# The second feed forward of a two-block model as seven block products per block, with the fifteen sums on VectorE

## The reference

```python
SEQ, D_MODEL, D_FF = 512, 1024, 4 * D_MODEL
for layer in range(2):
    ...
    h = _rmsnorm(x, norm_g[layer, 1]) * (1.0 + scale_f) + shift_f
    x = x + gate_f * (jnp.square(jax.nn.relu(h @ w_fc1[layer])) @ w_fc2[layer])
return _rmsnorm(x, norm_f)
```

## Time and profile before

| | us |
|---|---|
| median of 3 runs | 3584.62 |
| lowest, highest | 3583.39, 3584.72 |
| the profiled execution's own time | 3582.96 |
| its span in the profile | 3581.2 |
| TensorE busy | 3211.5 (90% of the span) |
| VectorE busy | 1821.2 (51%) |
| ScalarE busy | 697.5 (19%) |

### The profile page before, as it was taken

One profiled execution on the slowest core, in us unless ns is written; L12 is line 12 of the kernel. 1 busy time (PEld: TensorE's weight loads), 2 busy tenths in 40 slices (PEclk: granted clock), 3 DMA queues, 4 the chain that ended last, 5 costly groups with the idle time before them and its releaser, 6 DMA issues. The chain is left out here.

```text
span 3581.2 us, 27361 instructions
## 1 busy us (share of the span) xinstructions
PE 3211.5 (90%) x9960; PEld 1497.2 (42%) x9960; DVE 1821.2 (51%) x3995; ACT 697.5 (19%) x1519; POOL 653.9 (18%) x649
## 2 busy tenths in 40 slices
PE   8999799888888878787877899999999889999998
PEld 3454454333333333333333335444444475444443
DVE  5565831577766777677775237436544383111000
ACT  2133220222222222222221221112100232100000
POOL 0110100244444444444444000000000000000000
PEclk9999899999999899999899999999999999999999
DMA  5643411699999999999999122023444352112221
GB/s 196 233 159 105 153 59 59 257 422 417 421 407 406 421 421 422 421 421 421 412 418 418 67 112 71 36 85 115 184 158 145 148 207 98 62 66 75 80 73 71
DMA packets 118663, 799.00 MB, mean 223 GB/s; under 512 B 13728, under 2 KB 16416, under 8 KB 31872
## 3 DMA queue, kind: packets, MB, share of 16 engines
q0 software_dynamic: 91312, 619.09, 42.9%
q1 hardware_dynamic: 27216, 178.15, 13.7%
HBM read 767.83 MB, written 29.36 MB: 223 GB/s over the span
## 5 line engine op out<-in xcount | busy, mean ns | idle before, releaser
L1278 PE MATMUL po<-pair,diag 128*128 128x512 f32 x2048 | 988.1, 640 | 224.9 <-ACT diag L1338 224.7
L1425 DVE SCALAR_TENSOR_TENSOR pair<-pair,h_tm 128x1024 f32<-128x1024 f32 x512 | 616.2, 1224 | 298.7 <-DMA pair<-in_peer_uv,idx 295.2
L1198 POOL DMA_INDIRECT pair<-in_peer_uv,idx x512 | 581.5, 1136 | 964.1 <-PE po L1278 670.1
L1278 PEld LDWEIGHTS po<-pair,diag 128*128 128x128 f32 x2048 | 410.6, 205 | 781.5 <-issue 486.4
L1571 PE MATMUL acc<-a,ring 128*128 128x512 f32 x1024 | 441.7, 592 | 0.0
L1556 PE MATMUL acc<-hT,ring 128*128 128x512 f32 x960 | 412.3, 592 | 0.0
L1571 PEld LDWEIGHTS acc<-a,ring 128*128 128x128 f32 x1024 | 194.6, 190 | 244.9 <-issue 244.9
L1556 PEld LDWEIGHTS acc<-hT,ring 128*128 128x128 f32 x960 | 182.4, 190 | 229.6 <-issue 229.6
L1332 ACT ACTIVATE ge<-a 128x4 f32<-128x4 f32 x128 | 26.3, 205 | 895.9 <-DVE pair L1425 895.8
L1614 DVE SCALAR_TENSOR_TENSOR xT<-acc,mod,xT 128x512 f32<-128x512 f32 x16 | 12.0, 751 | 348.2 <-PE acc L1571 348.2
L1603 DVE TENSOR_TENSOR a<-a 128x512 f32<-128x512 f32 x64 | 43.6, 691 | 261.0 <-ACT a L1582 259.8
(11 more groups left out here) (405 smaller groups left out, 3213.3 us busy)
## 6 DMA issues: line engine op xcount, KB each, us to landing
ring<-in_w_fc SPq DMA_DIRECT2D x62, 1024.0 KB, 4.8
mg<-in_ada_w POOLq DMA_DIRECT2D x96, 512.0 KB, 5.2
s_tables<-table POOLq DMA_DIRECT2D x16, 1664.0 KB, 6.5
tab<-s_tables SPq DMA_DIRECT2D x16, 1664.0 KB, 6.4
ring<-in_w SPq DMA_DIRECT2D x15, 1024.0 KB, 4.9
first<-in_w_first SPq DMA_DIRECT2D x14, 1024.0 KB, 5.4
other<-in_w_first SPq DMA_DIRECT2D x14, 1024.0 KB, 5.0
pair<-in_peer_uv,idx POOLq DMA_INDIRECT x512, 14.6
```

The lines of the kernel that those rows point to most:

```text
L1198: pool.indirect_dma_start(out=pair[:, at, :], out_offset=None, in_=core.dram["peer_uv"][:, :], in_offset=bass.IndirectOffsetOnAxis(ap=idx[ ...
L1278: last = pe.matmul(po[:, t % 2, half * 512:(half + 1) * 512], diag[:, at, :], pair[:, at, D + half * 512:D + (half + 1) * 512], start=firs ...
L1425: dve.scalar_tensor_tensor(row, row, 1.0, h_tm[:, t, :], ALU.mult, ALU.mult, accum_out=a[:, g, s:s + 1]).then_inc(dotted, 1)
```

## The change

The stage is replaced by `feed_forward_halves`. Each product is treated as a product of 2x2 blocks: the weight matrix is halved by rows and by columns, the tokens' matrix is halved by features (tiles 0 to 3 and 4 to 7 of `hT`, or the two halves of a group of 8 tiles of `a`) and by tokens (0 to 255, `lo`, and 256 to 511, `hi`). Seven products of blocks take the place of eight. For that, four sums of weight blocks are made per chunk (`Halves.add`), four sums of token blocks per tile (`th` for the first product; `t` and, in place, the `hi` half of `a` for the second), and seven sums of results per tile. All of these run on VectorE. All matmuls of the stage have 256 columns.

One unit `p` of the first product is one chunk: seven groups of four matmuls, into two banks `x` and `y` of which each half is a result of its own. ScalarE copies `x` and `y` to `px` and `py` before the first half of each is accumulated further, and takes the third result straight into `a`. The ReLU moves into VectorE's squaring: `max(a, 0) * a`. In the second product four chunks make one unit `j`, which gives two output tiles, `j` and `4 + j`.

The weights are laid out on the host in another order (`by_halves`), again in chunks of 1 MB, and are issued by `Feed.load` (L341) by the same rule as before.

```diff
 class Sums:
...
-        act.activation(self.sq[:, k % 2, :], self.core.xT[:, k, :], ACT.Square).then_inc(self.squared, 1)
+        act.activation(self.sq[:, k % 2, :], self.core.xT[:, self.order[k], :], ACT.Square).then_inc(self.squared, 1)
...
+class Halves:
...
+    def add(self, dve, c):
+
+        if c >= 2:
+            dve.wait_ge(self.made, c - 1)
+        w = self.feed.chunk(dve, c, True)
+        a11, a12, a21, a22 = (w[:, i * 512:(i + 1) * 512] for i in range(4))
+        s = [self.sums[:, c % 2, i, :] for i in range(4)]
+        dve.tensor_tensor(s[0], a21, a22, ALU.add).then_inc(self.ready, 1)
+        dve.wait_ge(self.ready, 4 * c + 1)
+        dve.tensor_tensor(s[1], s[0], a11, ALU.subtract).then_inc(self.ready, 1)
+        dve.tensor_tensor(s[2], a11, a21, ALU.subtract).then_inc(self.ready, 1)
+        dve.wait_ge(self.ready, 4 * c + 2)
+        dve.tensor_tensor(s[3], a12, s[1], ALU.subtract).then_inc(self.ready, 1)
...
+def feed_forward_halves(core, layer, following):
+
+    N1, HT = FF // P, FF // P // 2
...
+        sums = Sums(core, st, st.ps("ms", [P, S])[:, :], sq=sq)
+        sums.order = [0, 4, 1, 5, 2, 6, 3, 7]
...
+        @block.tensor
+        def _(pe):
+            def seven(out, weight, tokens, first, start, stop=True):
+                for k in range(4):
+                    last = pe.matmul(out, weight(k), tokens(k), start=(start and k == 0), stop=(stop and k == 3), skip_group_check=True)
+                return last
+
+            for p in range(HT):
+                x, y = bank[:, 2 * (p % 2), :], bank[:, 2 * (p % 2) + 1, :]
...
+                feed.chunk(pe, p, True)
+                if p == 0:
+                    pe.wait_ge(products.ready, 4)
+                if p >= 2:
+                    pe.wait_ge(c_taken, p - 1)
+                seven(x[:, lo], block_(0), lambda k: core.hT[:, k, lo], True, True)
+                pe.wait_ge(halves.ready, 4 * p + 2)
+                if p == 0:
+                    pe.wait_ge(t_ready, 2)
+                seven(x[:, hi], sum_(2), lambda k: th[:, 1, k, :], True, False).then_inc(x_made, 1)
+                if p >= 2:
+                    pe.wait_ge(y_taken, p - 1)
+                seven(y[:, lo], sum_(1), lambda k: th[:, 0, k, :], True, True)
+                pe.wait_ge(halves.ready, 4 * p + 3)
+                if p == 0:
+                    pe.wait_ge(t_ready, 3)
+                seven(y[:, hi], sum_(3), lambda k: core.hT[:, k, hi], True, False).then_inc(y_made, 1)
+                pe.wait_ge(x_copied, p + 1)
+                seven(x[:, lo], block_(1), lambda k: core.hT[:, 4 + k, lo], False, False).then_inc(z_made, 1)
+                pe.wait_ge(halves.ready, 4 * p + 4)
+                pe.wait_ge(y_copied, p + 1)
+                seven(y[:, lo], sum_(4), lambda k: core.hT[:, 4 + k, hi], False, False)
+                if p == 0:
+                    pe.wait_ge(t_ready, 4)
+                seven(y[:, hi], block_(3), lambda k: th[:, 2, k, :], False, False).then_inc(made, 1)
+
+            for j in range(4):
...
+                for kk in range(4):
+                    n = HT + 4 * j + kk
...
+                    if kk == 0 and j >= 2:
+                        pe.wait_ge(x_copied, HT + j - 1)
+                        pe.wait_ge(y_copied, HT + j - 1)
+                        pe.wait_ge(z_copied, j - 1)
...
+                    if kk == 0 and j:
+                        pe.wait_ge(added, 2 * j)
+                    seven(last_half, block_(3), lambda k: t[:, 2, at + k, :], True, start).then_inc(made, 1)
+                    if kk == 1 and j:
+                        sums.add(pe, 2 * j - 2)
+                    if kk == 2 and j:
+                        sums.add(pe, 2 * j - 1)
+            sums.add(pe, KT - 2)
+            sums.add(pe, KT - 1)
+
+        @block.scalar
+        def _(act):
...
+            for p in range(HT):
...
+                act.wait_ge(x_made, p + 1)
+                if p:
+                    act.wait_ge(a_ready, p)
+                copy(px[:, :, :], two(x), x_copied)
+                act.wait_ge(y_made, p + 1)
+                copy(py[:, :, :], two(y), y_copied)
+                act.wait_ge(z_made, p + 1)
+                copy(a[:, p, lo], x[:, lo], c_taken)
...
+        @block.vector
+        def _(dve):
...
+            products.vector(dve)
+            halves.add(dve, 0)
+            h = core.hT
+            dve.wait_ge(products.ready, KT)
+            sub(th[:, 0, :, :], h[:, 0:4, hi], h[:, 0:4, lo]).then_inc(t_ready, 1)
+            dve.wait_ge(t_ready, 1)
+            sub(th[:, 1, :, :], h[:, 4:8, hi], th[:, 0, :, :]).then_inc(t_ready, 1)
+            sub(h[:, 0:4, hi], h[:, 4:8, hi], h[:, 0:4, hi]).then_inc(t_ready, 1)
+            dve.wait_ge(t_ready, 2)
+            sub(th[:, 2, :, :], h[:, 4:8, lo], th[:, 1, :, :]).then_inc(t_ready, 1)
+            for p in range(HT):
+                y = bank[:, 2 * (p % 2) + 1, :]
+                halves.add(dve, p + 1)
+                dve.wait_ge(x_copied, p + 1)
+                step.mark(dve.tensor_tensor(u1, px[:, 0, :], px[:, 1, :], ALU.add))
+                dve.wait_ge(y_copied, p + 1)
+                step(dve.tensor_tensor(v1, py[:, 0, :], py[:, 1, :], ALU.add))
+                step.mark(dve.tensor_tensor(a[:, HT + p, hi], u1, v1, ALU.add))
+                dve.wait_ge(made, p + 1)
+                step.mark(dve.tensor_tensor(a[:, p, hi], y[:, lo], u1, ALU.add))
+                dve.tensor_tensor(a[:, HT + p, lo], y[:, hi], u1, ALU.add).then_inc(y_taken, 1)
...
+                for f in (p, HT + p):
+                    step.mark(dve.scalar_tensor_tensor(a[:, f, :], a[:, f, :], 0.0, a[:, f, :], ALU.max, ALU.mult))
+                step.wait()
+                step(sub(t[:, 0, p, :], a[:, p, hi], a[:, p, lo]))
+                step.mark(sub(t[:, 1, p, :], a[:, HT + p, hi], t[:, 0, p, :]))
+                step(sub(a[:, p, hi], a[:, HT + p, hi], a[:, p, hi]))
+                sub(t[:, 2, p, :], a[:, HT + p, lo], t[:, 1, p, :]).then_inc(a_ready, 1)
+            for j in range(4):
+                for kk in range(4):
+                    n = HT + 4 * j + kk
+                    if kk < 3 or j < 3:
+                        halves.add(dve, n + 1)
+                dve.wait_ge(x_copied, HT + j + 1)
+                step(dve.tensor_tensor(u2, px[:, 0, :], px[:, 1, :], ALU.add))
+                dve.wait_ge(y_copied, HT + j + 1)
+                step.mark(dve.tensor_tensor(v2, u2, py[:, 0, :], ALU.add))
+                step(dve.tensor_tensor(u2, u2, py[:, 1, :], ALU.add))
+                dve.wait_ge(z_copied, j + 1)
+                step.mark(dve.tensor_tensor(c[:, 3, :], u2, py[:, 0, :], ALU.add))
+                step.mark(dve.tensor_tensor(c[:, 0, :], c[:, 0, :], px[:, 0, :], ALU.add))
+                step(dve.tensor_tensor(c[:, 1, :], c[:, 1, :], v2, ALU.add))
...
+                dve.scalar_tensor_tensor(core.xT[:, j, :], flat(0), gate(j), core.xT[:, j, :], ALU.mult, ALU.add).then_inc(added, 1)
+                dve.wait_ge(made, HT + 4 * j + 4)
+                step(dve.tensor_tensor(c[:, 2, :], bank[:, 3, lo if j % 2 else hi], u2, ALU.add))
+                dve.scalar_tensor_tensor(core.xT[:, 4 + j, :], flat(1), gate(4 + j), core.xT[:, 4 + j, :], ALU.mult, ALU.add).then_inc(added, 1)
...
-        feed_forward(core, 1, None)
+        feed_forward_halves(core, 1, None)
```

More of the change, by code:

```diff
@@ L277, in __init__ @@
     def __init__(self, core, st, ms, sq=None):
-        self.core, self.ms = core, ms
+        self.core, self.ms, self.order = core, ms, range(KT)
         self.sq = st.sb("sums_sq", [P, 2, S]) if sq is None else sq
@@ L1616, in _, with __init__, block, sum @@
                     vector_round(dve, 9 + j)
+class Halves:
+    def __init__(self, core, st, feed, made):
+        self.feed, self.made = feed, made
+        self.sums = st.sb("weight_sums", [P, 2, 4, 512])
+        self.ready, self.step = st.sem("sums_ready"), st.sem("sums_step")
+    def add(self, dve, c):
[10 more added lines that the diff above has]
+        dve.tensor_tensor(s[3], a12, s[1], ALU.subtract).then_inc(self.ready, 1)
+    def block(self, c, i, k):
+        w = core_first_or_ring(self.feed, c)
+        return w[:, i * 512 + k * P:i * 512 + (k + 1) * P]
+    def sum(self, c, i, k):
+        return self.sums[:, c % 2, i - 1, k * P:(k + 1) * P]
@@ L2500, in lay_out_more @@
     d["w2"] = by_chunks(np.concatenate(pairs + [w[:, 4 * MA:], f["w_out_2"][0]], 1), 256)
[L2501 to L2504, removed]
+    d["w_fc1_0"] = by_chunks(f["w_fc1_2"][0], 256)
+    w = f["w_fc2_2"][0].reshape(2, FF // 2, D)
+    d["w_fc2_0"] = np.concatenate([by_chunks(w[half, :, j * P:(j + 1) * P], P) for j in range(KT) for half in range(2)])
+    d["w_fc1_1"] = by_halves(f["w_fc1_2"][1])
+    d["w_fc2_1"] = by_halves(f["w_fc2_2"][1])
     pairs = [f[n][0][:, j * P:(j + 1) * P] for j in range(KT) for n in ("w_glu_b_2", "w_glu_a_2")]
@@ L2546, in by_chunks, with by_halves @@
```

(4 more changed lines are left out.)

81 lines of the change are left out of this document (added).

## The result

| | before | changed |
|---|---|---|
| median of 4 runs, us | 3584.64 | 3538.18 |
| lowest, highest | 3583.39, 3584.72 | 3535.74, 3543.11 |
| profiled execution, its span | 3582.96, 3581.2 | 3536.91, 3535.1 |
| stage: VectorE's first instruction to the final norm's first | 453.20 | 407.81 |
| VectorE's first instruction to the end of the last product | 448.73 | 402.12 |

The ratio is 0.9873, 95% interval 0.9856 to 0.9890. The forecast was 3540. The stage line is the one to compare by: it is 45.39 us shorter. The other 0.7 us of the spans' 46.1 lie ahead of the stage, where the code is the same (its start is at 3118.79 in place of 3119.52).

What follows compares the result with a forecast made beforehand. TensorE, busy throughout, was taken as the bound. Fewer matmul columns, less the start's idle and slow clock, end the last product 45.7 us earlier; 1.3 us lost at the end leaves -44.4: 3584.62 to 3540 us, range 3534 to 3553.

Steps and rivals of the forecast that it cites:

- The pitch: TensorE matmuls of the stage: 256-column records start 215.9 ns apart, taken from 32 records of another stage.
- VectorE's work in a unit costs nothing: First product: VectorE's 8.4 us hide within TensorE's 12.09 us unit, as a sum and as a chain.
- The margins: First product's units: ScalarE's copy of `x` is done 1.8 us before TensorE wants it, that of `y` 0.9.
- The price of being late: First product: each microsecond of lateness beyond a margin costs 16 us, once per unit.
- The start: Stage start: TensorE idles 3.4 us before the second group, then loses 2.2 us to the slow clock.
- The end: After the last product: the last square starts 1.3 us later than before, counted from that product.
- The sum: Whole stage: last product ends 45.7 us earlier; with 1.3 us at the end, net -44.4 us.
- Rival 1: TensorE's 190 ns weight load no longer fits the 216 ns pitch; fully exposed, 339 us more, 3879 us; chance 0.04.
- Rival 2: TensorE's waits expose one 0.19 us load at each of 223 groups: 42.4 us, 3582 us, no change; chance 0.03.
- Rival 3: Copies of `x` or `y` come late for TensorE; one microsecond over gives 16 us; 3548 to 3570 us, chance 0.10.

Runs made afterwards that it cites:

- the version with eight products of 256 columns: Kernel before, with each matmul of this stage split into two of 256 columns; stage 455.55 us against 453.20, whole time 3593.01 us.
- three times the sums: Changed kernel with eight more VectorE sums of 128x512 ahead of the four weight sums of each chunk; stage 419.02 us, whole time 3554.14 us.
- The version with 128 columns: Changed kernel with each 256-column matmul split into two of 128; stage 421.19 us against 407.81, whole time 3553.19 us.

## Why the prediction was right

- **The pitch.** The sum stood on 32 records of another stage. It held over 1792: 215.9 ns. No step of the sum weighs more, and the version with eight products of 256 columns shows it apart from the rest.
- **VectorE's work in a unit costs nothing.** Right, and the reason given (a chain, not a share) is the one that counts: the same instructions in another order cost 76 us. The margins were 2.1 and 0.92 us where 1.8 and 0.9 were forecast. Its busy time was put too high, 59% of a unit where two thirds were forecast. The price of being late was too low for a large lateness: I counted each microsecond over a margin once, and with 3.2 us per unit the clock took more than half of it again (5.0 us), while 0.4 us per unit cost 0.4.
- **The start.** Idle 3.48 us (3.4 forecast). At the slow clock 1.45 us in the profile of the result and 2.96 and 2.99 in the changed kernel's two others, where I took 2.2 within 0 to 2.7: right in the middle, but the upper bound was too low, taken from a single row.
- **The end.** 1.23 us for 1.3.
- **The sum.** -45.7 us to the last product was -46.6, counted from VectorE's first instruction, in the profile of the result, and -45.1 in the two others; the slow clock makes the difference between them. That the median of 3538 us came within 2 us of the forecast is in part luck: three medians of the changed kernel are 46.5, 41.7 and 41.1 us below the kernel before beside them, and the profiled executions spread by up to 9.8 us in the stages ahead, where nothing was changed.
- **Rival 1** had the wrong bound: 26 ns of slack, where the pitch goes on down to 112 ns. Its chance of 0.04 was too high for what a load costs.
- **Rival 2** is refuted by the version with a wait at each matmul. **Rival 3**'s mechanism exists and is the one by which this change could have lost everything, but in this order of instructions the margins hold in each unit.
- My later figure for three times the sums (+22 us, measured 11.2) failed because I took recorded durations for the pace, where starts one behind the other are closer than durations. That for 128 columns (+72, measured 13.4) rested on eight records that take 1.02 us from start to start (2902.63 to 2903.65) ahead of a matmul of another shape; another eight in the same trace take 0.87 (447.12 to 447.99), 109 ns each.

## What to carry to other kernels

Where TensorE is busy throughout and VectorE is idle, trading an eighth of the matmul columns for sums on VectorE can pay for the most part (here 44 to 45 of 52.6 us), if the sums that release TensorE's next wait stand ahead of those that are wanted later; look at the chain from the last matmul of a unit to the next wait, and not at VectorE's share. Here a stall of 3.2 us on TensorE in each unit cost 5, since the granted clock fell behind it; one of about 0.5 us cost no more than itself. Take the pace of matmuls and vector instructions from starts, from many records of one form, and never from recorded durations.

## What the runs showed of the hardware that I had not expected

- Weight loads of 128x128 fp32 blocks recorded with 192 ns follow each other every 112 ns and are hidden behind matmuls of 128 columns: 111.9 ns per record at 128 columns, 215.9 at 256, 429.2 at 512.
- Inside a dense stream, an idle time of 3.2 us on TensorE in each unit took the granted clock of the stretch from 1.00 to 0.90: 1.8 us lost behind each.
- After the single idle time at the stage's start the next 16 records lost 1.45 us once and 2.9 to 3.05 us five times, though the idle time was longer the once (3.48 against 3.02 to 3.07 us). The first group's eight records took 3.34 us in that profile at a granted clock of 0.58, and 3.75 at 0.50 in the other five. The version with 128 columns sides with the one: 3.46 us at 0.56, 3.36 idle, 1.5 lost. So at like idle times the smaller loss goes with a first group in which the clock had begun to rise; a longer idle time costs as well, for three times the sums has 3.42 us at 0.58, 8.47 idle and 2.4 lost:

```profile
3128.41 3.42 PE L1690 MATMUL bank<-hT,first 128*128 128x256 f32 x8 [6.38 <-ACT hT L308]
3140.29 6.02 PE L1690 MATMUL bank<-th,weight_sums 128*128 128x256 f32 x16 [8.47 <-DVE th L1805]
```

Why the clock rises within the first group in one execution and not in another, no run shows.
